# Four attentions: the mask is added by VectorE while it finds each row's maximum, instead of by products of TensorE

## The reference

```python
# first block: 8 differential heads (two score maps each, one taken from the other)
p = masked_softmax(q @ k^T * scale, key <= query)            # "diff"
# first block, native sparse attention: 4 groups of 4 heads; with 512 tokens
# the selected blocks and the window both come to the causal mask
p = masked_softmax(q @ k^T * scale, key <= query)            # "nsa", for ks/vs and for kw/vw
# second block, layer A: 16 heads with forget gates
p = softmax(q @ k^T * scale + c_q - c_k, key <= query)       # "fox"
# second block, layer B: 16 query heads over 4 key heads, window 128, one sink logit a head
p = softmax(concat(q @ k^T * scale where 0 <= query-key < 128, sink))[:-1]   # "swa"
```

## Time and profile before

| | us |
|---|---|
| median of 3 runs | 1768.23 (1767.32 to 1769.28) |
| the profiled execution, its own time | 1767.02 |
| span of the profile | 1765.2 |
| PE busy | 1678.9 (95%) |
| DVE busy | 934.0 (53%) |
| ACT busy | 726.6 (41%) |
| POOL busy | 383.9 (22%) |
| mask products: L2263 | 128 instructions, mean 233 ns |
| mask products: L2381 | 480 instructions, mean 222 and 234 ns |
| maxima on DVE | 320 instructions, 81.3 + 57.0 us |

### The profile page before, as it was taken

The page is one execution under the profiler, slowest core; times in us unless marked ns, Lnnn a source line. Parts: engine busy times, 40 slices in busy tenths (PEclk is TensorE's granted clock), DMA queues, the critical chain, the costliest instruction groups (busy, mean ns, idle before and its releaser), DMA issues.

```text
span 1765.2 us, 24732 instructions
## 1 busy us (share of the span) xinstructions
PE 1678.9 (95%) x9314; PEld 1318.3 (75%) x9314; DVE 934.0 (53%) x1675; ACT 726.6 (41%) x1643; POOL 383.9 (22%) x517
## 2 busy tenths in 40 slices
PE   7999998998879998999999999999999998998979
PEld 6887766887755555888888888888887767886757
DVE  3795664356246676345343234334745774457772
ACT  4334663153336666223332123233335553534550
POOL 5441332022115654011000000000112330023330
PEclk9999998999958999999999999999999998999989
DMA  7223002423012221423322232224231003230111
GB/s 187 81 87 96 25 25 84 143 74 128 14 34 58 67 59 36 153 96 96 95 96 95 96 96 96 95 96 134 83 109 35 26 25 139 77 96 25 49 49 48
DMA packets 107206, 141.38 MB, mean 80 GB/s; under 512 B 30349, under 2 KB 55205, under 8 KB 106849
## 3 DMA queue, kind: packets, MB, share of 16 engines
q1 hardware_dynamic: 106032, 139.10, 24.8%
q0 software_dynamic: 992, 0.86, 0.5%
q10 hardware_dynamic: 80, 0.02, 0.0%
HBM read 125.24 MB, written 4.24 MB: 73 GB/s over the span
## 4 chain that ended last, share of the span: by engine, by line
PE 66%; DVE 11%; issue 10%; ACT 9%; POOL 3%; DMA 0%; ACTq 0%; SPq 0%; POOLq 0%; DVEq 0%
PE ps L2023 51%; PE ps L2477 2%; PE ps L2258 2%; DVE spl L1171 2%; DVE nm L1500 2%; ACT pbd L954 2%; PE ps L2279 2%; PE ps L2294 1%; PE ps L2432 1%; ACT pb L898 1%; ACT qkt L975 1%; PE ps L2456 1%; ACT pts L962 1%; ACT pbs L954 1%; DVE qkt L1518 1%
## 5 line engine op out<-in xcount | busy, mean ns | idle before, releaser
L2023 PE MATMUL ps<-spl,ht 128*128 128x512 f32 x2496 | 579.5, 394 | 9.2 <-DVE xk L1709 5.9
L2023 PEld LDWEIGHTS ps<-spl,ht 128*128 128x128 f32 x2496 | 473.4, 190 | 109.3 <-DVE xk L1709 6.3
L1194 DVE TENSOR_TENSOR spl<-raw,spl 128x1024 fp32r<-128x1024 f32 x168 | 222.2, 1364 | 396.8 <-ACT spl L726 396.8
L726 ACT ACTIVATE spl<-raw 128x1024 fp32r<-128x1024 f32 x168 | 168.5, 1052 | 464.1 <-PE ps L2023 437.7
L2023 PE MATMUL ps<-ht,spl 128*128 128x512 f32 x960 | 220.4, 391 | 2.0 <-DVE spl L1194 2.0
L2023 PEld LDWEIGHTS ps<-ht,spl 128*128 128x128 f32 x960 | 181.1, 189 | 40.6 <-issue 2.9
L2023 PE MATMUL ps<-spl,uu 128*128 128x512 f32 x768 | 174.7, 389 | 0.0
L2023 PEld LDWEIGHTS ps<-spl,uu 128*128 128x128 f32 x768 | 144.1, 188 | 29.9
L2477 PE MATMUL ps<-ht,spl 128*128 128x512 f32 x576 | 155.2, 408 | 2.7 <-DVE mx L1555 2.6
L2477 PEld LDWEIGHTS ps<-ht,spl 128*128 128x128 f32 x576 | 102.7, 190 | 23.8 <-DVE mx L1555 4.8
L1885 POOL TENSOR_TENSOR sq_first<-qkv 128x2048 f32<-128x2048 f32 (+1 forms) x14 | 47.9, 3423 | 316.0 <-ACT qkv L769 301.4
(11 more groups left out here) (315 smaller groups left out, 2228.2 us busy)
## 6 DMA issues: line engine op xcount, KB each, us to landing
raw<-w_in SPq DMA_DIRECT2D x30, 1024.0 KB, 5.1
raw<-w_mlp_up SPq DMA_DIRECT2D x16, 1024.0 KB, 5.2
raw<-w_mlp_down SPq DMA_DIRECT2D x16, 1024.0 KB, 5.1
raw<-w_in_a SPq DMA_DIRECT2D x16, 1024.0 KB, 5.3
raw<-w_in_b SPq DMA_DIRECT2D x8, 1024.0 KB, 5.3
raw<-w_proj_diff SPq DMA_DIRECT2D x4, 1024.0 KB, 6.2
stq<-qkv SPq DMA_DIRECT2D x16, 256.0 KB, 2.7
stq<-qkv SPq DMA_DIRECT2D x32, 128.0 KB, 2.5
```

What stands on the lines that cost most here:

```text
L726: act.activation(SPL[:, n % 2, HI, 2 * k:2 * k + 2], RAW[:, n % 2, 2 * k:2 * k + 2], ACT.Copy).then_inc(hi_done, 4)
L1194: dve.tensor_tensor(SPL[:, n % 2, LO, 2 * k:2 * k + 2], RAW[:, n % 2, 2 * k:2 * k + 2], SPL[:, n % 2, HI, 2 * k:2 * k + 2].bitcast(F32), A ...
L2023: last = pe.matmul(PS[:, b0 + b], left[:, x], right[:, y], start=(kt == 0 and i == 0), stop=(kt == UK * g["units"] - 1 and i == 2))
```

## The change

PE's mask products go, all 608 of them. The scores' last product (in fox the decay's) now releases the scores. DVE's maximum becomes one operation (`tensor_tensor_reduce`) that reads the scores in PSUM and a mask of bf16 in SBUF, adds them, multiplies by -1, writes the result back over the scores, and keeps the smallest value of the row in `NM`. It compiles to two instructions, the operation itself and one that reads the accumulator out. ACT computes exp(-1 x (negated masked score) + `NM`). The masks now are as wide as the scores: `CAUSAL` of 512 columns, of which the last `w` are used, and `BAND` of 2 x 128 + 2.

In nsa one wait for both heads' scores takes the place of a wait for each, and it hangs on a copy of one column (`SEEN`). Elsewhere each head still has its own wait. POOL makes fewer masks: its list of fills and selects is shorter ahead of the small loads.

```diff
@@ -32,6 +32,7 @@
 HD = 64
 EPS = 1e-6
 MASKED = -1e30
+LARGE = 3e38
 LAMBDA_INIT = 0.2
 FF = 4096
 CMP_BLOCK, CMP_STRIDE = 32, 16
@@ -313,8 +314,7 @@
         PC = region("pc", "sc", [GROUPS, S], plus=16 * KB)
 
         IDF, IDB = sb("idf", [P]), sb("idb", [P], BF16)
-        CAUSAL = sb("causal", [P], BF16)
-        ID64, CAUSAL64, BAND64 = [sb(x, [2, P], BF16) for x in ("id64", "causal64", "band64")]
+        CAUSAL, BAND = sb("causal", [S], BF16), sb("band", [2 * P + 2], BF16)
         ONES = sb("ones", [P])
         COS, SIN = sb("cos", [NT, HD // 2]), sb("sin", [NT, HD // 2])
         CT, ST = sb("ct", [2, NT, HD]), sb("st", [2, NT, HD])
@@ -338,6 +338,7 @@
         CMA, CMB, CM1 = sb("cma", [NT, 32]), sb("cmb", [NT, 32], BF16), sb("cm1", [NT])
         LC = region("lc", "sc", [4, GROUPS * NT * 4], plus=27 * KB)
         RST = sb("rst", [4, NT])
+        SEEN = sb("seen", [2, NT])
         EPSC, MINUS_HALF = sb("epsc", [1]), sb("minus_half", [1])
         GT = sb("gt", [NT, 48])
         FL = region("fl", "sc", [8, NT, 16], plus=24 * KB)
@@ -477,6 +478,11 @@
         def diff_output(half, k):
 
             return NWS[:, :, YD[half] + P * k:YD[half] + P * k + P]
+
+        def mask_of(a, t):
+
+            w = a.width(t)
+            return BAND[:, 2 * P - w:2 * P + a.sink] if a.banded else CAUSAL[:, S - w:S]
 
         def by_tile(x):
 
@@ -896,7 +902,7 @@
                         act.wait_ge(s["mx"], 8 * m.n + 2 * idx + h + 1)
                         p = PB[:, m.slot, h, a.offset(t):a.offset(t) + w]
                         last = act.activation(p, PS[:, 2 * (idx % 2) + h, 0:w], ACT.Exp, bias=NM[:, m.slot, h, t:t + 1],
-                                              accum_out=LS[:, m.slot, h, t:t + 1])
+                                              scale=-1.0, accum_out=LS[:, m.slot, h, t:t + 1])
                     last.then_inc(s["e"], 1)
 
                 def turned(m, j):
@@ -952,7 +958,7 @@
                     for h in range(2):
                         act.wait_ge(*need(a, "mx", 2 * n + h + 1))
                         last = act.activation(PBS[a.name][n % 3][:, h, 0:w], PS[:, score_bank(a, n, h), 0:w], ACT.Exp,
-                                              bias=NM[:, m % 2, h, t:t + 1], accum_out=LS[:, m % 2, h, t:t + 1])
+                                              bias=NM[:, m % 2, h, t:t + 1], scale=-1.0, accum_out=LS[:, m % 2, h, t:t + 1])
                     last.then_inc(s["e"], 1)
 
                 def turned(n):
@@ -1413,11 +1419,12 @@
                 def maxima(m, t):
                     idx = NT - 1 - t
                     w = a.width(t)
+                    dve.wait_ge(s["s"], 8 * m.n + 2 * idx + 2)
+                    dve.tensor_copy(SEEN[:, m.slot, t:t + 1], ONES[:, 0:1])
                     for h in range(2):
-                        n = 8 * m.n + 2 * idx + h + 1
                         bank, top = PS[:, 2 * (idx % 2) + h], NM[:, m.slot, h, t:t + 1]
-                        dve.wait_ge(s["s"], n)
-                        dve.tensor_reduce(top, bank[:, 0:w], AX.X, ALU.max, negate=True).then_inc(s["mx"], 1)
+                        dve.tensor_tensor_reduce(bank[:, 0:w], bank[:, 0:w], mask_of(a, t), -1.0, LARGE, ALU.add, ALU.min,
+                                                 top).then_inc(s["mx"], 1)
 
                 def norms(m, t):
                     idx = NT - 1 - t
@@ -1497,8 +1504,8 @@
                             dve.tensor_scalar(bank[:, w:w + 1], SINK[:, 2 * m + h:2 * m + h + 1], 1.0, None, ALU.mult)\
                                .then_inc(sink_in, 1)
                             dve.wait_ge(sink_in, 2 * n + h + 1)
-                        dve.tensor_reduce(NM[:, m % 2, h, t:t + 1], bank[:, 0:w + a.sink], AX.X, ALU.max, negate=True)\
-                           .then_inc(s["mx"], 1)
+                        dve.tensor_tensor_reduce(bank[:, 0:w + a.sink], bank[:, 0:w + a.sink], mask_of(a, t), -1.0, LARGE,
+                                                 ALU.add, ALU.min, NM[:, m % 2, h, t:t + 1]).then_inc(s["mx"], 1)
 
                 def norms(n):
                     m, i = divmod(n, NT)
@@ -1579,6 +1586,7 @@
                     scaled_tile(k)
                 for m, i in a.first_turns()[3:]:
                     low(m, i)
+                dve.wait_ge(consts, 14)
                 maxima(0)
                 for k in range(a.lead):
                     gate(k)
@@ -1812,31 +1820,25 @@
             pool.memset(IDF[:], 0.0).then_inc(consts, 1)
             pool.memset(IDB[:], 0.0).then_inc(consts, 1)
             pool.memset(CAUSAL[:], 0.0).then_inc(consts, 1)
-            pool.memset(ID64[:], 0.0)
-            pool.memset(BAND64[:], 0.0).then_inc(consts, 1)
-            pool.memset(CAUSAL64[:], 0.0).then_inc(consts, 1)
+            pool.memset(BAND[:, 0:P], 0.0).then_inc(consts, 1)
+            pool.memset(BAND[:, P:2 * P + 2], 0.0).then_inc(consts, 1)
             pool.wait_ge(consts, 5)
             for m in (IDF, IDB):
                 pool.affine_select(out=m[:], in_=m[:], compare_op=ALU.not_equal, fill=1.0, base=0,
                                    pattern=[[-1, P]], channel_multiplier=1).then_inc(consts, 1)
 
-            pool.affine_select(out=CAUSAL[:], in_=CAUSAL[:], compare_op=ALU.is_ge, fill=MASKED, base=0,
+            pool.affine_select(out=CAUSAL[:, S - P:S], in_=CAUSAL[:, S - P:S], compare_op=ALU.is_ge, fill=MASKED, base=0,
                                pattern=[[-1, P]], channel_multiplier=1).then_inc(consts, 1)
 
             pool.memset(ONES[:], 1.0 / P).then_inc(consts, 1)
             pool.memset(EPSC[:], EPS).then_inc(consts, 1)
             pool.memset(KBD[:], 0.0).then_inc(consts, 1)
             pool.memset(ONEB[:], 1.0).then_inc(consts, 1)
-            for h in range(2):
-                r = slice(HD * h, HD * h + HD)
-                pool.wait_ge(consts, 12 + h)
-                pool.affine_select(out=ID64[r], in_=ID64[r], compare_op=ALU.not_equal, fill=1.0, base=0,
-                                   pattern=[[HD, 2], [-1, P]], channel_multiplier=1)
-                pool.affine_select(out=CAUSAL64[r], in_=CAUSAL64[r], compare_op=ALU.is_ge, fill=MASKED, base=0,
-                                   pattern=[[HD, 2], [-1, P]], channel_multiplier=1)
-                last = pool.affine_select(out=BAND64[r], in_=BAND64[r], compare_op=ALU.is_ge, fill=MASKED, base=-1,
-                                          pattern=[[-HD, 2], [1, P]], channel_multiplier=-1)
-                last.then_inc(consts, 1)
+            pool.wait_ge(consts, 12)
+            pool.affine_select(out=BAND[:, 0:P], in_=BAND[:, 0:P], compare_op=ALU.is_ge, fill=MASKED, base=-1,
+                               pattern=[[1, P]], channel_multiplier=-1).then_inc(consts, 1)
+            pool.affine_select(out=BAND[:, P:2 * P], in_=BAND[:, P:2 * P], compare_op=ALU.is_ge, fill=MASKED, base=0,
+                               pattern=[[-1, P]], channel_multiplier=1).then_inc(consts, 1)
             pool.wait_ge(consts, 14)
 
             small = []
@@ -2255,13 +2257,11 @@
                     for i, (x, y) in enumerate(((HI, HI), (HI, LO), (LO, HI))):
                         for h in range(2):
                             r = slice(HD * h, HD * h + HD)
-                            pe.matmul(PS[:, 2 * (idx % 2) + h, 0:w], QKT[r, m.slot, 0, x, P * t:P * t + P],
-                                      QKT[r, m.slot, 1, y, P * a.first_key(t):P * t + P],
-                                      start=(i == 0), stop=False, skip_group_check=True)
-                    for h in range(2):
-                        bank = PS[:, 2 * (idx % 2) + h]
-                        pe.matmul(bank[:, w - P:w], IDB[:], CAUSAL[:], start=False, stop=True,
-                                  skip_group_check=True).then_inc(s["s"], 1)
+                            last = pe.matmul(PS[:, 2 * (idx % 2) + h, 0:w], QKT[r, m.slot, 0, x, P * t:P * t + P],
+                                             QKT[r, m.slot, 1, y, P * a.first_key(t):P * t + P],
+                                             start=(i == 0), stop=(i == 2), skip_group_check=True)
+                            if i == 2:
+                                last.then_inc(s["s"], 1)
 
                 def copies(m, idx, extra):
 
@@ -2361,27 +2361,16 @@
                     for j, (x, y) in enumerate(((HI, HI), (HI, LO), (LO, HI))):
                         for h in range(2):
                             r = slice(HD * h, HD * h + HD)
-                            pe.matmul(PS[:, score_bank(a, n, h), 0:w], QKT[r, m % 2, 0, x, P * t:P * t + P],
-                                      QKT[r, a.keys_of(m) % 2, 1, y, P * a.first_key(t):P * t + P],
-                                      start=(j == 0), stop=False, skip_group_check=True)
+                            last = pe.matmul(PS[:, score_bank(a, n, h), 0:w], QKT[r, m % 2, 0, x, P * t:P * t + P],
+                                             QKT[r, a.keys_of(m) % 2, 1, y, P * a.first_key(t):P * t + P],
```

(18 more changed lines are left out.)

## The result

The changed kernel takes 1770.38 us (median of 12 runs, 1769.14 to 1772.18), the kernel before on the same chip 1766.56 us (12 runs, 1765.46 to 1769.28). The ratio is 1.0020, with a 95% interval of 1.0011 to 1.0028: slower by 2 to 5 us, not faster by 7. The profiled execution has a span of 1768.4 us, where the one before had 1765.2. The time lies inside the range of the forecast; the sign was wrong.

A forecast was written before the change was run, and what follows sets the result against it. The prediction took PE to lead in nsa, ACT and DVE in diff and swa, with fox between. Gains of 5.0 + 1.5 + 0.5 + 0.3 = 7.3 us gave 1760.9 us from 1768.23, range 1752 to 1774.

The forecast's parts named there:

- By this row the second instruction is free: 0: DVE's maxima: the accumulator's read ends when the main instruction ends, so it adds 0 us.
- the second rival: DVE's second instruction is paid, 9 us on the chain against 7.3 gained: 1769.9 us, no change; chance 0.16.
- The upper end: DVE's accumulator read: 0.08 us in series for each of 112 maxima on the chain, 9 us.
- Nsa's gain on PE: Mask products leaving nsa's chain: 0.31 us a unit, for 16 units 5.0 us.
- The lower end: Nsa's gain with 0.08 taken off a unit for the accumulator: 0.23 x 16 = 3.7 us.
- 0.23 us at 568.65: A piece of mask on nsa's chain, not counted, since 0.22 us of slack keeps ACT from starting earlier.
- Fox: Mask pieces of 0.11 and half of 0.16 us leave the chain: 0.19 x 8 = 1.5 us gained.
- Diff and swa: Few mask pieces on the chain, where ACT and DVE lead: 0.3 us gained in diff, 0.5 in swa.
- Rival 3: The write back to PSUM halves DVE's pace, 1.75 times a reduction's time: +31 us, 1792; chance 0.07.
- Rival 4: In nsa an idler PE stays at 1.2 GHz: +35 us, small form +3 to +10; chance 0.10, small form 0.04.
- the signs named for each step: Profile signs of error, among them diff's maximum-to-exp distance grown by 0.08, or a shorter diff or swa.
- The rule that the prediction sets against the earlier trace: DVE's pipe is flushed after each operation before the next starts, so the number of operations counts, against a free second instruction.

The follow-up runs named there:

- E6: Changed kernel, but in diff, fox and swa DVE's operation writes to SBUF and exp reads it there: 1771.66 us against 1767.53 for the kernel before.
- E1: Changed kernel with PE's 608 mask products put back, adding zeros, so DVE's half alone: 1777.57 us against 1767.24 for the kernel before, +10.3 us.
- e2: Changed kernel with no mask added anywhere and DVE's old reduction, so PE's half alone: 1760.64 us against 1767.24 for the kernel before, -6.6 us.
- e5: Changed kernel, but in swa both heads' sinks are written ahead of both maxima: 1767.70 us against 1767.53 for the kernel before.
- e4: Changed kernel with six idle PE products a step in the last units of diff, fox and swa: 1767.82 us against 1767.24 for the kernel before.
- e9: Changed kernel with PE's masks and the old reduction back in diff, fox and swa, nsa alone new: 1764.29 us against 1767.52 for the kernel before.
- e11: Kernel before with six idle PE products a step in the last units of diff, fox and swa: 1763.62 us against 1767.52 without them, -3.9 us.
- e10: Kernel of e8 with 18 more idle products, 8 ahead of nsa's first unit and 10 in it: 1756.99 us against 1767.52 for the kernel before.
- e8: Kernel of e9 with idle products in the last units of diff, fox and swa, and swa's sinks first: 1760.98 us against 1767.53 for the kernel before.

## Why the prediction was wrong, step by step

| stage, us | forecast | period after - before, times units |
|---|---|---|
| diff | -0.3 | +0.27 x 8 = +2.2 |
| nsa | -5.0 | -0.22 x 16 = -3.5 |
| fox | -1.5 | +0.08 x 8 = +0.6 |
| swa | -0.5 | +0.50 x 8 = +4.0 |
| sum | -7.3 | +3.3 (the time: +3.8) |

The table takes every unit at the period of the middle ones. From the first exp to the end of the last, in the two profiles, diff grew by 3.2 us, nsa shrank by 1.9, fox grew by 0.1 and swa by 3.5, in all 4.9, and the stretches around them gave back 1.7. First units differ from one profile to the next, as the clock does. So it is in part luck that 3.3 comes so near to 3.8.

- **The step that failed** is "By this row the second instruction is free: 0". The row was that of an operation that writes 64 columns to SBUF. E6 shows the row to be right for SBUF. E1 shows what all of DVE's half is worth here: 10.3 us, in which the copy of one column in nsa has about 16 x 0.07 = 1.1. PE's half was forecast nearly right, 7.3 us against 6.6 (e2). So the mechanism is that of the second rival, to which I gave 0.16. Its size, 9 us, was nearly right in sum and not in its parts: 2.6 for each of diff, fox and swa and 1.3 for nsa, where e1 has 2.2, 1.5, 4.1 and 3.0. That its time of 1769.9 is so near to 1770.38 is luck: it stands 1.7 us above 1768.23, the measured time 3.8 above 1766.56. Prediction and row agree on where the read-out starts; its length was the open number, and I had written that the write to PSUM was shown by no row. From the sink's 151 ns I took that such a write costs nothing extra at its start. It does not, for itself; what pays is the read-out behind it, 139 ns against 81.
- **The upper end counted one maximum a step.** In swa both heads are in the ring, since exp of the second head waits for its own maximum, and the sink's write pays as well (e5). Swa alone lost 4.0 us where 32 x 0.08 = 2.6 had been the bound.
- **Nsa's gain on PE was right.** 0.31 us a unit was 0.22 and 0.16 of products less 0.07 for the copy; e2, which has no copy, shows those 0.38. The lower end, 0.23 with the read-out paid, is what came: 0.22. That 0.23 us at 568.65 is worth nothing agrees with this sum, and no run takes it apart. Of e1's 0.19 in nsa, the copy (0.07) and the later exp (0.06 to 0.08) explain about 0.14; the rest is open.
- **Fox** gives 0.12 a unit on PE (e2; forecast 0.19), and DVE's half takes 0.19 (e1).
- **Diff and swa** gain nothing on PE (forecast 0.3 and 0.5): e2 leaves both at their period. PE's masks did not hold them.
- **Rival 3** is out: 714 against 686 ns at 512 columns, 1.04 times and not 1.75, and 684 ns into SBUF.
- **Rival 4** came in its small form. After 536.4 us the clock rises later than before, this row against one of 0.90 in the kernel before; nsa as a whole stays at 0.93 (0.94 in the earlier trace rows):

```profile
536.40:547.00 10.60, 10.60 (x56) 6.51 (x54) 5.74 (x21) 5.73 (x18) 4.83 (x8) 0.68 0.20 49
```

  Nsa's second unit lasts 13.51 us instead of 12.17, which takes back 1.3 of the 3.5 us that the middle units give. But the same nsa code has a second unit of 12.12 us in e4 and 11.86 in e9 (there the stretch is at 0.95), so the late rise is not a matter of that code alone. It does not set the sign. With the idle products in both, the change costs 4.5 us (e4 is at +0.6, e11 at -3.9 against the kernel before), and 3.8 without them. And e2, in which PE has as few products as after, gains 6.6 us where its units say 7.0.

Of the signs named for each step, two told it at once: diff's distance from maximum to exp grew by 0.08 (0.77 to 0.85), and diff and swa changed length by more than 1 us.

The Trainium skill has differences of this size ("Perfetto Trace Analysis", "Optimizing Scalar/DVE Operations"): an access of DVE costs some 60 ns on SBUF and some 125 ns on PSUM, one of ScalarE some 93 ns on SBUF and some 51 on PSUM, and it says that the profiled latency is about twice that. The rows have 58 ns for the read-out (139 behind an output in PSUM, 81 behind one in SBUF) and 33 ns for exp (715 from SBUF, 682 from PSUM), near the simple differences of 65 and 42 and not near their double. That the instruction behind a write to PSUM pays, and not only the write, is what e6 shows. With this difference in view, rival 2 would have deserved more than 0.16.

The rule that the prediction sets against the earlier trace rows ("VectorE: DVE Perf Modes", "The DRAIN you can't avoid" in the Trainium skill) goes on to say that a next operation that is not held starts earlier. The rows agree: after the change too the read-out starts at 204.03, before the operation ends at 204.11. The read-out is paid, but not because a flush comes ahead of it.

## What to carry to other kernels

An operation that also gives its accumulator is two instructions, and the second one's length depends on where the first one writes; take its price from a row with the same destination, and multiply it by every place where someone waits for the accumulator, both heads of a step if both are waited for. Moving work off TensorE paid only in the stage where TensorE sets the pace: it was worth 3.5 us in nsa, less in fox than what it cost there, and nothing in diff and swa, where the engine that takes the work over was in the ring already. So cost such a change by stage, and make it by stage.

## What the runs showed of the hardware

- The read-out of DVE's accumulator takes 139 to 142 ns behind an operation that writes PSUM (320 instances) and 81 ns behind one that writes SBUF (192), and a one-column write to PSUM takes 0.21 us right behind a read-out of the first kind (32 of 32), 0.15 to 0.16 behind one of the second kind (e6) and 0.15 elsewhere.
- Products that compute nothing make this kernel faster. In stretches where TensorE has little to do they hold the granted clock at 1.00: at the ends of diff, fox and swa, where it was 0.85, 0.80 and 0.76 (35 us each), for -3.9 us (e11), and at the start of nsa, where it was 0.50, for about -4 us (e10 against e8).
